# Waits outside the first unit of a layer: who makes a low part, where a guard stands, and how many dense pieces stand on which side of a chunk loop

## What is computed

```python
def hybrid_layer(x, norm_g, w_in, conv_w, a_log, dt_bias, dn_g, w_up_r, w_up_d, w_o):
    proj = rmsnorm(x, norm_g) @ w_in
    (rq, rk, rv, rz, dq, dk, dv, dz, db, da, gr, gd) = jnp.split(proj, _split_points(), axis=-1)
...
    o_r = retention(rope(rq), rope(rk) * RET_DK ** -0.5, rv)
    o_r = (o_r - mu) * lax.rsqrt(var + EPS) * jax.nn.silu(rz)
    qkv = jax.nn.silu(causal_conv(concat(dq, dk, dv), conv_w))
...
    o_d = gated_deltanet(l2norm(q) * DN_DK ** -0.5, l2norm(k), v, sigmoid(db), g)
    o_d = o_d * lax.rsqrt(mean(o_d * o_d) + EPS) * dn_g * jax.nn.silu(dz)
    y = sigmoid(gr) * (o_r @ w_up_r) + sigmoid(gd) * (o_d @ w_up_d)
    return x + y @ w_o
```

## Time and profile before

| what | value |
|---|---|
| time, median of 3 runs | 2701.21 us (2700.89 to 2704.86) |
| time of the profiled execution | 2703.87 us |
| its span, first to last instruction | 2702.1 us |
| PE busy | 2654.9 us, 98% |
| DVE, POOL, ACT busy | 1647.2, 836.1, 626.2 us |
| mean granted TensorE clock | 0.998 of full speed |
| dense matmuls of 128 by 512 (L746, L748, L750) | 2560 each from the activations |

### The profile page before, as it was taken

The page is one execution under the profiler, slowest core; times in us unless marked ns, Lnnn a source line. Parts: engine busy times, 40 slices in busy tenths (PEclk is TensorE's granted clock), DMA queues, the critical chain, the costliest instruction groups (busy, mean ns, idle before and its releaser), DMA issues.

```text
span 2702.1 us, 39281 instructions
## 1 busy us (share of the span) xinstructions
PE 2654.9 (98%) x14674; PEld 2260.2 (84%) x14674; DVE 1647.2 (61%) x3718; ACT 626.2 (23%) x1261; POOL 836.1 (31%) x459
## 2 busy tenths in 40 slices
PE   7999999999999999999999999999999999999998
PEld 6888888888888888888878888888888888888886
DVE  7878777877744443434587778777877434443333
ACT  5333333333211101200142333333322111120001
POOL 3233333333321212434522333333332122232443
PEclk9999999999999999999999999999999999999999
DMA  4321222122211112433532222222222111133344
GB/s 169 95 87 52 84 63 87 52 84 64 83 42 39 48 35 70 124 100 116 157 95 81 74 78 61 74 73 80 60 78 65 42 49 42 40 107 98 94 140 140
DMA packets 292832, 217.79 MB, mean 81 GB/s; under 512 B 31682, under 2 KB 246036, under 8 KB 292388
## 3 DMA queue, kind: packets, MB, share of 16 engines
q1 hardware_dynamic: 254322, 151.21, 19.6%
q10 hardware_dynamic: 38322, 64.07, 7.1%
HBM read 176.37 MB, written 38.86 MB: 80 GB/s over the span
## 4 chain that ended last, share of the span: by engine, by line
PE 85%; DVE 7%; DMA 2%; POOL 2%; issue 2%; ACT 1%; SPq 1%; ACTq 0%; DVEq 0%; POOLq 0%
PE dense_ps L746 21%; PE dense_ps L750 20%; PE dense_ps L748 20%; PE work L729 3%; PE dense_ps L770 2%; PE dense_ps L771 2%; PE dense_ps L772 2%; PE work L1002 1%; DMA arena<-l_scratch 1%; PE work L961 1%; PE work L1039 1%; PE work L978 1%; PE work L1059 1%; PE work L1028 1%; PE work L1052 1%
## 5 line engine op out<-in xcount | busy, mean ns | idle before, releaser
L746 PE MATMUL dense_ps<-act_hi,w_hi 128*128 128x512 f32 x2560 | 1063.6, 415 | 6.2 <-DVE w_lo L2110 2.4
L750 PE MATMUL dense_ps<-act_hi,w_lo 128*128 128x512 f32 x2560 | 1002.5, 392 | 0.0
L748 PE MATMUL dense_ps<-act_lo,w_hi 128*128 128x512 f32 x2560 | 1000.1, 391 | 0.0
L2230 POOL TENSOR_TENSOR w_lo<-w_raw,w_hi 128x1024 fp32r<-128x1024 f32 x164 | 404.7, 2468 | 1072.1 <-ACT w_hi L1264 565.2
L750 PEld LDWEIGHTS dense_ps<-act_hi,w_lo 128*128 128x128 f32 x2560 | 480.6, 188 | 106.3
L746 PEld LDWEIGHTS dense_ps<-act_hi,w_hi 128*128 128x128 f32 x2560 | 482.9, 189 | 91.0 <-DVE w_lo L2110 2.9
L748 PEld LDWEIGHTS dense_ps<-act_lo,w_hi 128*128 128x128 f32 x2560 | 483.4, 189 | 81.6 <-issue 0.5
L1726 DVE SCALAR_TENSOR_TENSOR arena<-arena,cols 128x512 f32<-128x512 f32 x288 | 241.3, 838 | 5.1
L1581 DVE CAST w_hi<-w_raw 128x1024 fp32r<-128x1024 f32 x90 | 63.7, 708 | 187.8 <-PE dense_ps L772 112.7
L729 PE MATMUL work<-mk,arena 128*128 128x128 f32 x768 | 113.4, 277 | 13.3 <-issue 7.5
L1740 DVE SCALAR_TENSOR_TENSOR arena<-arena 128x512 f32<-128x512 f32 x96 | 112.8, 1175 | 13.2 <-ACT arena L1270 13.1
(11 more groups left out here) (217 smaller groups left out, 3807.9 us busy)
## 6 DMA issues: line engine op xcount, KB each, us to landing
w_raw<-in_w_in SPq DMA_DIRECT2D x138, 512.0 KB, 3.8
gate_scratch<-arena ACTq DMA_DIRECT2D x64, 256.0 KB, 2.3
arena<-gate_scratch ACTq DMA_DIRECT2D x64, 256.0 KB, 3.2
arena<-l_scratch SPq DMA_DIRECT2D x62, 256.0 KB
w_raw<-in_w_out SPq DMA_DIRECT2D x18, 512.0 KB, 4.2
o_scratch<-arena ACTq DMA_DIRECT2D x32, 256.0 KB, 2.0
arena<-o_scratch ACTq DMA_DIRECT2D x32, 256.0 KB, 3.6
w_raw<-in_w_up_dn SPq DMA_DIRECT2D x16, 512.0 KB, 4.2
```

Source lines behind the costliest of these rows:

```text
L746: eng.matmul(dense_ps[:, to, :], w_hi[:, slot, k, :], hi[:, k, seg], start=(k == 0), stop=False)
L748: eng.matmul(dense_ps[:, to, :], w_hi[:, slot, k, :], lo[:, k, seg], start=False, stop=False)
L750: mm = eng.matmul(dense_ps[:, to, :], w_lo[:, slot, k, :], hi[:, k, seg], start=False, stop=(k == KT - 1))
L2230: eng.tensor_tensor(w_lo[:, slot, :, :], w_from[second][:, :, :], w_hi[:, slot, :, :].bitcast(F32), ALU.subtract)\
```

## The change

It moves steps between engines and within their orders; nothing is computed otherwise. In the order of the kernel: the step "qe" goes from slot 5 to slot 10 in all units but the first. At the start of layer 1 the gate pieces and key pieces of the second half alternate from the first tile on, ACT evicts earlier, and DVE makes the low parts of the even tiles and POOL those of the odd ones (in layer 0 it stays the other way round). In the retention heads, hf = 0 has four pieces ahead of the chunk products and nine behind them. The wait for `ob_ok` goes into the first head, ahead of the output transposes. The first output block of the second half waits for only its own low parts, where before the first block of all waited for both halves' low parts. `norm_rows` of layer 1's first half goes two pieces back. ACT's rounding of the second up-projection weight goes ahead of the o_d roundings, DVE's low part of it ahead of `od_low(1)`, and POOL waits for it ahead of its own low parts. ACT makes the high part of the second output block, and POOL its low part ahead of the last low part of y. DVE makes the low part of the first head's second value weight.

```diff
@@ -163,8 +163,8 @@
...
         at(4, "qt")
-        at(5, "qe")
         at(7, "kq")
+        at(10, "qe")
         solve, spread_at, vt = 3, 8, 19
...
@@ -893,11 +893,12 @@
...
                     next(gates1)
-                    if k >= 2:
+                    if l or k >= 2:
                         next(keys1)
...
                     pass
-                next(keys1)
+                if l == 0:
+                    next(keys1)
                 eng.wait_ge(b_row.sem, b_row.after(l, 2))
...
@@ -1110,7 +1111,7 @@
...
                         mm.then_inc(rsc_ps.sem, 1)
-                        fill(5 if hf == 0 else 2)
+                        fill(4 if hf == 0 else 2)
                         eng.wait_ge(rkd_ok.sem, rkd_ok.after(t, hf + 1))
...
@@ -1130,7 +1131,7 @@
...
                             mm.then_inc(ro_ps.sem, 1)
-                            fill(1 if c < CPH - 1 else 8)
+                            fill(1 if c < CPH - 1 else 9 if hf == 0 else 8)
                         for _ in fills:
...
@@ -1141,6 +1142,8 @@
...
                         eng.wait_ge(ron_ok.sem, ron_ok.after(t, hf + 1))
+                        if h == 0 and hf == 0:
+                            eng.wait_ge(ob_ok.sem, ob_ok.after(l * (2 * DH) + (2 * DH - 1), 1))
                         for e in range(2):
...
@@ -1150,7 +1153,6 @@
...

-                eng.wait_ge(ob_ok.sem, ob_ok.after(l * (2 * DH) + (2 * DH - 1), 1))
                 for h in range(RH - 1):
...
@@ -1164,10 +1166,10 @@
...
                                           order=n + BLK_OUT + i // 2,
-                                          ready=(lambda b, k: (yl_ok.sem, yl_ok.after(l * KT + k, 2))) if i == 0 else None)
+                                          ready=(lambda b, k: (yl_ok.sem, yl_ok.after(l * KT + k, b + 1))) if i in (0, KT) else None)
                     for k in range(KT):
                         next(pieces)
-                        if more and i == KT + 3 and k == 3:
+                        if more and i == KT + 3 and k == 5:
                             norm_rows(l + 1, 0)
...
@@ -1278,11 +1280,13 @@
...

+                if l:
+                    raw_evac(n, l * DH, 0)
                 for k in range(KT):
                     norm_hi(l, 1, k)
-                    if k == 1:
+                    if l == 0 and k == 1:
                         raw_evac(n, l * DH, 0)
-                    if k == 2:
+                    if k == 2 - l:
                         gates_evac(0)
...
@@ -1517,10 +1521,10 @@
...

+                split_hi(n + BLK_UPD + 1, (BLK_UPD + 1) % 2)
                 for i in range(KT, 2 * KT):
...
                     if i == KT + 2:
-                        split_hi(n + BLK_UPD + 1, (BLK_UPD + 1) % 2)
                         for b in range(NHALF):
...
@@ -1534,6 +1538,7 @@
...
                     gate_load(f)
+                split_hi(n + BLK_OUT + 1, (BLK_OUT + 1) % 2)

...
@@ -1597,7 +1602,14 @@
...
                     eng.wait_ge(dense_ok[1].sem, dense_ok[1].after(g - j + 1 - 6, 1))
-                eng.tensor_copy(v_weights(h)[0][:, :, j * P:(j + 1) * P], w_raw[:, :, :]).then_inc(w_hi_ok.sem, 1)
+                hi, lo = v_weights(h)
+                col = slice(j * P, (j + 1) * P)
+                eng.tensor_copy(hi[:, :, col], w_raw[:, :, :]).then_inc(w_hi_ok.sem, 1)
+                if h == 0 and j == 1:
+                    eng.wait_ge(w_hi_ok.sem, w_hi_ok.after(g, 1))
+                    eng.wait_ge(w_lo_ok.sem, w_lo_ok.after(g, 0))
+                    eng.tensor_tensor(lo[:, :, col], w_raw[:, :, :], hi[:, :, col].bitcast(F32), ALU.subtract)\
+                       .then_inc(w_lo_ok.sem, 1)

...
@@ -1636,7 +1648,7 @@
...
                 eng.tensor_tensor(act_lo[:, k, seg], hfull[:, k % HBUF, :], act_hi[:, k, seg].bitcast(F32), ALU.subtract)\
-                   .then_inc(n_lo[1].sem, 1)
+                   .then_inc(n_lo[k % 2].sem, 1)

...
@@ -1709,9 +1721,12 @@
...
                     norm_apply(l, 1, k)
-                    if k >= 2 and k % 2 == 0:
+                    if k >= 2 and k % 2 == l:
                         norm_lo(l, 1, k - 1)
-                norm_lo(l, 1, KT - 1)
+                    elif l and k == 1:
+                        norm_lo(l, 1, 0)
+                if l == 0:
+                    norm_lo(l, 1, KT - 1)

...
@@ -2103,12 +2118,12 @@
...
                         else:
-                            od_low(1)
                             g, slot = n + BLK_UPD + 1, (BLK_UPD + 1) % 2
...
                                               ALU.subtract).then_inc(w_lo_ok.sem, 1)
+                            od_low(1)
                             od_low(3)
...
@@ -2172,9 +2187,10 @@
...

-                split_w(n + BLK_OUT + 1, (BLK_OUT + 1) % 2)
                 for i in range(NHALF * KT):
                     b, j = i // KT, i % KT
+                    if i == 0:
+                        eng.wait_ge(w_hi_ok.sem, w_hi_ok.after(n + BLK_OUT + 2, 0))
                     if not more and i >= KT + 6:
...
@@ -2249,7 +2265,7 @@
...
                 eng.tensor_tensor(act_lo[:, k, seg], hfull[:, k % HBUF, :], act_hi[:, k, seg].bitcast(F32), ALU.subtract)\
-                   .then_inc(n_lo[0].sem, 1)
+                   .then_inc(n_lo[k % 2].sem, 1)

...
@@ -2277,7 +2293,7 @@
...
                 n = l * NBLK
-                for k in range(0, KT, 2):
+                for k in range(l, KT, 2):
                     norm_lo(l, 1, k)
...
@@ -2296,9 +2312,9 @@
...
                             idx = g0 + step[1] + 1
-                            if is_v(idx):
-                                split_v(l, 0, idx - BLK_RET - 2)
-                            elif kind != "first":
+                            if idx == BLK_RET + 2 and kind == "even_last":
+                                split_v(l, 0, 0)
+                            elif kind != "first" and not is_v(idx):
                                 split_w(g + idx, idx % 2)
...
@@ -2361,6 +2377,7 @@
...
                 ret_head(RH - 1, True)
+                eng.wait_ge(w_lo_ok.sem, w_lo_ok.after(n + BLK_UPD + 1, 1))
                 for k in LOW_POOL:
...
@@ -2371,10 +2388,11 @@
...
                         seg = slice(b * HALF, (b + 1) * HALF)
+                        if j == KT - 1 and b == 1:
+                            split_w(n + BLK_OUT + 1, (BLK_OUT + 1) % 2)
                         eng.wait_ge(yh_ok.sem, yh_ok.after(l * KT + j, b + 1))
...
                                           ALU.subtract).then_inc(yl_ok.sem, 1)
-                split_w(n + BLK_OUT + 1, (BLK_OUT + 1) % 2)
                 more = l + 1 < DEPTH
...
                     split_w(n + BLK_OUT + i + 2, i % 2, i % 2 == 0)
```

## The result

The changed kernel took 2712.91 us (median of 5 runs, 2712.28 to 2714.28), the kernel before 2701.21 (5 runs, 2700.89 to 2704.86). The ratio is 1.0035, with a 95% interval of 1.0023 to 1.0047: slower, by some 9.5 us by the ratio and 11.7 by the two medians. The time lies 0.9 above the end of the range, and beside rival 1, which gave 2710.6. The two profiled executions took 2703.87 and 2712.28, 8.4 apart.

The account below looks back on a forecast made before the run. TensorE (PE), busy 98% of the span, was taken as the bound, so its waits count. Removed waits -12.2, retention heads +10.4 and qe 0 sum to -1.8 us against the median 2701.21: 2699.4, no change; range 2689 to 2712.

Parts of the forecast that it names:

- rival 1: Even units: POOL goes first at the port, ahead of DVE's tap; +11.2 us, so 2710.6 us in all; chance 0.30.
- qe in the even units: qe in slot 10, fourteen even units: DVE's tap gets through before POOL, cost 0; +11.2 us if POOL goes first.
- The retention heads: Heads with hf = 0: eighth gate piece, tanh and z_silu come 1.30 us later, delaying the output; +10.4 us, eight places.
- The removed waits: PE's waits that the edits (a) to (g) take away or shorten: -12.2 us together.
- (a): Layer 1's first half: row sums two pieces back remove PE's wait on L1622; -1.36 us, once.
- (b): v_first's second low part goes from POOL to DVE, removing two waits of L770; -2.0 us.
- (c): First retention head: the ob_ok guard moves to the bank's first use, removing two waits on L2027; -2.0 us.
- (d): Second output block: POOL's subtraction goes before y's last low part, removing two waits of L2230; -1.9 us, bound 0.
- (e): End of retention: w_lo ahead of an o_d low part shortens two waits on L2110; -2.2 us, bounds -2.7 and +1.
- (f): Layer 1's start: low parts swap between DVE and POOL, gate pieces first; -0.1 us, bounds -0.8 and +0.5.
- (g): qe leaves slot 5 for slot 10 in fifteen units a layer, removing waits for L1995; -2.6 us, bound 0.

Follow-up runs that it names:

- the counterpart: Changed kernel with qe's reduction back in slot 5 and only its short instruction in slot 10: 2714.63 us, ratio 1.0040 to the kernel before.
- qe split: Changed kernel with qe's reduction kept in slot 10 and its short second instruction moved to slot 13: 2702.67 us, ratio 0.9998 to the kernel before.

## Why the prediction was wrong

**One term failed: qe in the even units.** The step reads "I take 0, as DVE's tap would be the earlier by some hundredths". In the record the tap was the earlier, 576.21 against 576.23, and POOL went first all the same; in the counterpart it was 579.46 against 579.49. The prediction's own price for this, 0.8 us in 14 units and 11.2 in all, is what was measured (11.2). With it in place of 0 the sum is -1.8 + 11.2 = +9.4, and rival 1 was right. (The prediction has the tap end at 575.2 in that case, where its own terms give 573.40 + 1.13 + 0.55 = 575.08; 575.08 - 574.22 - 0.06 is still 0.80.) Rival 1 should have been the likelier, as the nearest rows for it stood in the unit itself: of the two taps in the earlier trace rows the first got the port when POOL's instruction ahead of the masks ended, at 571.68,

```profile
569.30 2.38 POOL L2230 TENSOR_TENSOR w_lo<-w_raw,w_hi 128x1024 fp32r<-128x1024 f32 x1 [10.98 <-ACT w_hi L1264]
```

and POOL's L2308 got it before the second tap, although that stood directly behind the first. I weighed the outcome of L1788 from another stage against this, where the handover came out both ways. The price was worked out rightly and the order was not; why the order comes out so is open (last section).

**The retention heads** were right in mechanism and size: +10.4 forecast, 13.9 - 3.5 = +10.4 measured. z_silu in DVE's chain is shown by moving it, and the size by taking the two fills back (some 11 us).

**The removed waits.** (a), (b), (c), (d): none of these waits is in the list after; for the row sums only a wait of 1.0 in layer 0 is left, which the change does not touch. (e): no wait on w_lo is left; two short ones, 0.3 + 0.32 us in all, stand ahead of a piece of the first up-projection blocks (1103.23 in layer 0). The profile names nothing that they wait for; if they are a little of what the bound of +1 was for, (e) brought about -2.1 for the forecast -2.2. (f), forecast at -0.1, between the same two points:

```profile
1363.72 1.12 PE L805 MATMUL work<-arena,mk 128*128 128x512 f32 x2
...
1380.60 0.80 PE L962 MATMUL work<-arena 128*128 128x128 f32 x2 [1.70 <-DVE arena L1767]
```

16.88 us after, 16.96 before (1360.06 to 1377.02): -0.08. (g) holds in every profiled execution: with the reduction in slot 10 no wait on L1995's successor appears, in six profiles; with it in slot 5 there were three to seven, in four. Its size differs by run, as the prediction said, and the time of the kernel before ranges from 2700.65 to 2707.54. Where the kernel before had few such waits, (g) would bring less than its 2.6. That may be one reason why the medians differ by 11.7 and the profiles by 8.4, but how much of the spread of before is due to these loads was not measured.

**The range** ended at rival 1's centre plus 1.4, and was too short for a rival with a chance of 0.30 and a spread of its own.

The Trainium skill, "SBUF — State Buffer", section "Who interferes with whom", was taken to mean that the tap goes first if it issues first. The trace agrees that the one blocks the other for a whole instruction (the tap took 1.84 us with POOL's 1.27 ahead of it), but by the recorded starts the order was the other way round. The tap's recorded start (576.21) lies before the end of the instruction ahead of it (576.29), so the record need not show when it asked for the port.

## What to carry to other kernels

Before more pieces go behind a loop, ask which of them closes a PSUM bank, and who waits for that bank: here the eighth piece went behind the loop, and since DVE had the gate's wait in the middle of its statistics, the later bank cost more than the ninth piece covered. Where an instruction is put between two users of a shared port, ask who is waiting when it ends: here 0.16 us of DVE's own work cost PE 0.8. And a step that is moved out of a tight place should be moved instruction by instruction; here only the reduction had to go, and the rest belonged elsewhere.

## What was not expected of the hardware

An instruction of 128x4 that takes 0.16 us where nothing blocks it cost PE 0.8 us in each of fourteen units. Three runs show who got the port at this place. With qe split, the tap stood waiting when POOL's first mask ended (573.86 and 574.50) and went ahead of the second, which took 1.73. In the changed kernel and the counterpart the tap stood behind the short instruction and lost the port to POOL's second mask (taps at 576.21 and 579.46, 1.84 us each), even with an earlier recorded start.

This does not hold everywhere. At the end of retention in layer 0 of the changed kernel, DVE, then POOL:

```profile
1097.18 1.28 DVE L1803 TENSOR_TENSOR act_lo<-arena,act_hi 128x512 fp32r<-128x512 f32 x2
```

```profile
1097.34 3.54 POOL L2383 TENSOR_TENSOR act_lo<-arena,act_hi 128x512 fp32r<-128x512 f32 x2 [2.53 <-DVE w_lo L2124]
```

POOL's first L2383 stood from 1097.34 on, yet the second L1803, directly behind the first, was not held up (0.68 us each). That L2383 took 2.28 us, where the next took 1.29. What sets the two places apart was not tested, and the two outcomes of L1788 remain open as well.
